# Second layer of a four-layer decoder: 258 and then 256 token columns, where 272 were computed, behind its mixer

## What is computed

```python
def conv_ffn(h, w_up, conv_w, conv_b, w_down):          # FFN_CONV = 3 taps
    u = causal_depthwise_conv(h @ w_up, conv_w) + conv_b
    gate, up = u[..., :FFN_DIM], u[..., FFN_DIM:]       # FFN_DIM = 2816
    return (jax.nn.silu(gate) * up) @ w_down

def first_block(...):
    hs = jnp.concatenate([pad, meta, x], 1)             # 48 zero rows, 16 meta, 256 tokens
    for i in range(DEPTH):                              # DEPTH = 2
        a_in = rms_norm(hs, norm_w[i, 0])
        mix = gated_deltanet(...) if i % N_MIXERS == 0 else mlstm(...)
        hs = hs + keep * rms_norm(mix, norm_w[i, 1])
        f = conv_ffn(rms_norm(hs, norm_w[i, 2]), ...)
        hs = hs + keep * rms_norm(f, norm_w[i, 3])
    return hs[:, N_PAD + N_META:]                       # only the 256 tokens of x
```

## Time and profile before

| | |
|---|---|
| median of 3 runs | 1613.73 us (1612.49 to 1618.56) |
| the profiled execution | 1615.01 us |
| its span, first to last instruction | 1612.9 us |
| TensorE matmul busy | 1500.3 us, 93% |
| TensorE weight loads busy | 1437.5 us, 89% |
| VectorE busy | 1052.0 us, 65% |
| ScalarE busy | 802.5 us, 50% |
| GpSimd busy | 253.7 us, 16% |
| mean granted TensorE clock | 0.958 |
| moved by DMA | 222.54 MB, mean 138 GB/s |

### The profile page before, as it was taken

How to read it: one execution, slowest core, us unless ns; L and a number is a source line. 1 busy time by engine, 2 the same in 40 slices (tenths; PEclk the granted TensorE clock), 3 DMA queues, 4 the chain that set the end, 5 groups by cost and what they waited for, 6 DMA issues and landing times.

```text
span 1612.9 us, 32565 instructions
## 1 busy us (share of the span) xinstructions
PE 1500.3 (93%) x11741; PEld 1437.5 (89%) x11741; DVE 1052.0 (65%) x1769; ACT 802.5 (50%) x1390; POOL 253.7 (16%) x307
## 2 busy tenths in 40 slices
PE   6999969899999999999999998999999956999997
PEld 5997868698999989898999988999999945999996
DVE  4884874647887367558886377666656663666654
ACT  5655532436655365456664354454444642454443
POOL 0202200201554000002553000021100001021100
PEclk9998976999999999999999999999999975999998
DMA  5552320053555535233655542455554710265551
GB/s 199 180 172 75 102 69 1 1 170 107 192 175 179 172 107 179 92 118 120 193 170 182 173 141 92 144 172 183 184 180 142 225 40 0 92 194 183 182 182 53
DMA packets 61141, 222.54 MB, mean 138 GB/s; under 512 B 6784, under 2 KB 7808, under 8 KB 60672
## 3 DMA queue, kind: packets, MB, share of 16 engines
q1 hardware_dynamic: 60912, 220.17, 42.6%
q10 hardware_dynamic: 144, 1.18, 0.2%
HBM read 220.28 MB, written 1.05 MB: 137 GB/s over the span
## 4 chain that ended last, share of the span: by engine, by line
PE 81%; DVE 10%; ACT 6%; issue 2%; DMA 1%; POOL 0%; ACTq 0%; DVEq 0%; SPq 0%
PE bank L396 22%; PE bank L397 21%; PE bank L398 21%; DVE wlo L377 2%; ACT whi L372 2%; PE bank L415 1%; PE bank L416 1%; PE bank L422 1%; PE bank L561 1%; PE bank L1875 1%; ACT sq L578 1%; PE bank L1216 1%; DMA par<-params 1%; PE bank L1196 1%; DVE y L2113 1%
## 5 line engine op out<-in xcount | busy, mean ns | idle before, releaser
L377 DVE TENSOR_TENSOR wlo<-raw,whi 128x1024 fp32r<-128x1024 f32 x412 | 515.8, 1253 | 308.7 <-ACT whi L372 307.4
L372 ACT ACTIVATE whi<-raw 128x1024 fp32r<-128x1024 f32 x412 | 434.5, 1056 | 377.0 <-PE bank L398 363.7
L396 PE MATMUL bank<-xs,whi 128*128 128x272 f32 (+2 forms) x2080 | 600.1, 289 | 13.6 <-DVE wlo L377 11.9
L397 PE MATMUL bank<-xs,whi 128*128 128x272 f32 (+2 forms) x2080 | 595.6, 286 | 0.0
L398 PE MATMUL bank<-xs,wlo 128*128 128x272 f32 (+2 forms) x2080 | 593.3, 285 | 0.0
L396 PEld LDWEIGHTS bank<-xs,whi 128*128 128x128 f32 x2080 | 394.1, 189 | 18.0 <-issue 13.4
L398 PEld LDWEIGHTS bank<-xs,wlo 128*128 128x128 f32 x2080 | 394.8, 190 | 0.0
L397 PEld LDWEIGHTS bank<-xs,whi 128*128 128x128 f32 x2080 | 394.5, 190 | 0.1
L396 PE MATMUL bank<-hf,whi 128*128 (+2 forms) x1024 | 293.9, 287 | 10.9 <-issue 5.0
L397 PE MATMUL bank<-hf,whi 128*128 (+2 forms) x1024 | 292.9, 286 | 0.0
L398 PE MATMUL bank<-hf,wlo 128*128 (+2 forms) x1024 | 292.5, 286 | 0.0
(11 more groups left out here) (454 smaller groups left out, 1489.9 us busy)
## 6 DMA issues: line engine op xcount, KB each, us to landing
raw<-stream SPq DMA_DIRECT2D x412, 512.0 KB, 3.6
con<-consts SPq DMA_DIRECT2D x1, 1284.5 KB, 7.8
big<-mla ACTq DMA_DIRECT2D x1, 1152.0 KB, 5.5
hs_sb<-hs SPq DMA_DIRECT2D x1, 1088.0 KB, 5.1
y_out<-hs_sb SPq DMA_DIRECT2D x8, 128.0 KB, 2.0
par<-params SPq DMA_DIRECT2D x1, 644.0 KB, 8.9
```

The costliest lines, as they stand in the source:

```text
L372: nc.scalar.activation(whi[:, s, :], raw[:, s, :], ACT.Copy).then_inc(hi_split, 1)
L377: nc.vector.tensor_tensor(wlo[:, s, :], raw[:, s, :], whi[:, s, :].bitcast(F32), ALU.subtract).then_inc(block_split, 1)
L396: nc.tensor.matmul(out_, whi[:, slot, w], hi, start=start, stop=False)
L397: nc.tensor.matmul(out_, whi[:, slot, w], lo, start=False, stop=False)
```

## The change

The second layer's parts behind its mixer leave out columns that nothing reads later. `FIRST_TOKEN` gives a first column to three phases: 14 to `ml_out` and `up1` (the 256 tokens and the two that the convolution looks back to), 16 to `down1`. Matmuls, norms, splits and the residual addition around them take the columns from there to 271. From the SiLU on, and for GpSimd's product and split, it is 16 to 271. All tensors keep their places and sizes: the operands start at a later column of the same rows. For every other phase the first column is 0. The matmuls of `keep_clock` keep their size and read columns that start at 16.

Counted in the two programs, every engine has as many instructions as before and in the same order; only the widths of the ones above differ (on TensorE 1056 + 192 matmuls from 272 to 258 columns and 528 from 272 to 256, beside the sums).

```diff
+    CONV_HALO = 2
+    FIRST_TOKEN = {"ml_out": N_META - CONV_HALO, "up1": N_META - CONV_HALO, "down1": N_META}
+    POST_FIRST = {"post0": 0, "post1": 0, "post2": FIRST_TOKEN["ml_out"], "post3": FIRST_TOKEN["down1"]}
+    PRE_FIRST = {"pre1": 0, "pre2": 0, "pre3": FIRST_TOKEN["up1"]}
+    FFN_FIRST = (0, FIRST_TOKEN["up1"], 0, 0)
+    FFN_OUT = (0, FIRST_TOKEN["down1"], 0, 0)
+
+    def cols(phase):
+        return slice(FIRST_TOKEN.get(phase, 0), width(phase))
...
     def rhs_out(g, phase):
-        return bank[g % 8][:, 0:width(phase)]
+        return bank[g % 8][:, cols(phase)]
...
-                last = three(rhs_out(g, phase), (b0 + j) % SLOTS, k, xs[:, k, 0:T], xs[:, KC + k, 0:T], k == 0, k == KC - 1)
+                last = three(rhs_out(g, phase), (b0 + j) % SLOTS, k, xs[:, k, T], xs[:, KC + k, T], k == 0, k == KC - 1)
...
-        T = T1 if b0 < FIRST_BLOCK["ev_in"] else T2
+        T = cols(phase)
...
-                last = three(rhs_out(g0 + m, phase), (b0 + k) % SLOTS, m, hf[:, up + at, 0:T], hf[:, up + lo, 0:T], k == 0, k == n - 1)
+                last = three(rhs_out(g0 + m, phase), (b0 + k) % SLOTS, m, hf[:, up + at, T], hf[:, up + lo, T], k == 0, k == n - 1)
...
-            nc.scalar.activation(sq[:, m, :], bank[(g - 8 + m) % 8][:, 0:T1], ACT.Square).then_inc(*S("norm", "act").mark(f"{name}_{m}"))
+            nc.scalar.activation(sq[:, m, lo:T1], bank[(g - 8 + m) % 8][:, lo:T1], ACT.Square).then_inc(*S("norm", "act").mark(f"{name}_{m}"))
...
-        nc.vector.tensor_tensor(hs[:, m, :], hs[:, m, :], y[:, m, :], ALU.add).then_inc(*v.mark(f"{name}_h{m}"))
+        nc.vector.tensor_tensor(hs[:, m, t], hs[:, m, t], y[:, m, t], ALU.add).then_inc(*v.mark(f"{name}_h{m}"))
...
-                ins = nc.vector.scalar_tensor_tensor(o[:, tap:T1], bk[:, 0:T1 - tap], w[:, taps - 1 - tap:taps - tap],
-                                                     o[:, tap:T1], ALU.mult, ALU.add)
+                ins = nc.vector.scalar_tensor_tensor(o[:, lo + tap:T1], bk[:, lo:T1 - tap], w[:, taps - 1 - tap:taps - tap],
+                                                     o[:, lo + tap:T1], ALU.mult, ALU.add)
...
-                u = tiles[a][0][:, 0:T]
-                nc.vector.tensor_tensor(u, u, rs[:, 0, 0:T], ALU.mult).then_inc(*st.mark(f"u{f}_{base}_{j}{a}"))
+                u = tiles[a][0][:, FFN_FIRST[f]:T]
+                nc.vector.tensor_tensor(u, u, rs[:, 0, FFN_FIRST[f]:T], ALU.mult).then_inc(*st.mark(f"u{f}_{base}_{j}{a}"))
...
-            nc.tensor.matmul(bank[g % 8][:, 0:T2], hf[:, lo, 0:P], hf[:, lo + 1, 0:T2], start=True, stop=True)
+            nc.tensor.matmul(bank[g % 8][:, 0:T2], hf[:, lo, t:t + P], hf[:, lo + 1, t:t + T2], start=True, stop=True)
```

More of the change, by code:

```diff
@@ L402, in pe_tiles @@
         b0, n = FIRST_BLOCK[phase], count or COUNT[phase]
-        T = width(phase)
+        T = cols(phase)
         mm = nc.tensor.matmul
@@ L414, in pe_tiles @@
                         pe.wait_ge(bank_free, g0 + j + 1)
-                    mm(o, whi[:, s, w], xs[:, k, 0:T], start=(k == 0), stop=False)
-                    mm(o, wlo[:, s, w], xs[:, k, 0:T], start=False, stop=False)
+                    mm(o, whi[:, s, w], xs[:, k, T], start=(k == 0), stop=False)
+                    mm(o, wlo[:, s, w], xs[:, k, T], start=False, stop=False)
             if k:
@@ L421, in pe_tiles @@
                 for j in range(AHEAD):
-                    last = mm(rhs_out(g0 + j, phase), whi[:, (b0 + j) % SLOTS, w], xs[:, KC + k - 1, 0:T], start=False, stop=(k == KC))
+                    last = mm(rhs_out(g0 + j, phase), whi[:, (b0 + j) % SLOTS, w], xs[:, KC + k - 1, T], start=False, stop=(k == KC))
                     if k == KC:
@@ L496, in pe_sum, with act_scale @@
         last.then_inc(*S("norm", "pe").mark(name))
-    def act_scale(act, name, g, dst, T, count, eps):
+    def act_scale(act, name, g, dst, T, count, eps, lo=0):
         act.wait_ge(*S("norm", "pe").at(name))
-        nc.scalar.activation(dst, bank[g % 8][:, 0:T], ACT.Ln, bias=eps, scale=1.0 / count).then_inc(bank_free, 1)
+        nc.scalar.activation(dst, bank[g % 8][:, lo:T], ACT.Ln, bias=eps, scale=1.0 / count).then_inc(bank_free, 1)
         act.wait_ge(bank_free, 8 + g + 1)
@@ L546, in build, with keep_clock, sums_pe @@
     FIRST_SUM = 3
-    def keep_clock(pe, g, n, lo=0):
+    def keep_clock(pe, g, n, lo=0, t=0):
         pe.wait_ge(bank_free, g + 1)
         for _ in range(n):
-            nc.tensor.matmul(bank[g % 8][:, 0:T2], hf[:, lo, 0:P], hf[:, lo + 1, 0:T2], start=True, stop=True)
-    def sums_pe(pe, name, src, g, parts, T):
+            nc.tensor.matmul(bank[g % 8][:, 0:T2], hf[:, lo, t:t + P], hf[:, lo + 1, t:t + T2], start=True, stop=True)
+    def sums_pe(pe, name, src, g, parts, T, lo=0):
         for m, first, last_one in parts:
@@ L560, in sums_pe @@
             pe.wait_ge(*S("norm", who).at(mark))
-            last = nc.tensor.matmul(bank[g % 8][:, 0:T], ones, ap, start=first, stop=last_one)
+            last = nc.tensor.matmul(bank[g % 8][:, lo:T], ones, ap, start=first, stop=last_one)
         if last_one:
@@ L565, in post_src @@
     def post_src(name):
+        lo = POST_FIRST[name]
         def src(m):
-            return ("dve", f"{name}_sum{FIRST_SUM - 1}", sq[:, 0, :]) if m == 0 else ("act", f"{name}_{m}", sq[:, m, :])
+            return ("dve", f"{name}_sum{FIRST_SUM - 1}", sq[:, 0, lo:T1]) if m == 0 else ("act", f"{name}_{m}", sq[:, m, lo:T1])
         return src
@@ L677, in last_act, with conv_first @@
                 split_hi(act, fourth("ev_in"))
-    def conv_first(steps_, tag, tiles, taps, a):
+    def conv_first(steps_, tag, tiles, taps, a, lo=0):
         bk, slot, w = tiles[a]
@@ L685, in conv_first, with conv_rest @@
             args["bias"] = w[:, taps:taps + 1]
-        nc.scalar.activation(cv[:, slot, :], bk[:, 0:T1], ACT.Identity, **args).then_inc(*steps_.mark(f"{tag}{a}"))
-    def conv_rest(dve, steps_, first, tag, tiles, i, taps):
+        nc.scalar.activation(cv[:, slot, lo:T1], bk[:, lo:T1], ACT.Identity, **args).then_inc(*steps_.mark(f"{tag}{a}"))
+    def conv_rest(dve, steps_, first, tag, tiles, i, taps, lo=0):
         for tap in range(1, taps):
@@ L776, in pair @@
             if f < 2:
-                conv_rest(dve, st, a_, f"f{f}_{base}_{j}", tiles, i, 3)
+                conv_rest(dve, st, a_, f"f{f}_{base}_{j}", tiles, i, 3, FFN_FIRST[f])
                 split_lo(dve, b0 + t + 1 + TAIL, ii)
@@ L787, in ffn_pool @@
     def ffn_pool(pool, f, g0):
-        st, T = S("ffn", "pool"), T1 if f < 2 else T2
+        st, t = S("ffn", "pool"), slice(FFN_OUT[f], T1 if f < 2 else T2)
         def pair(j, i, base):
```

60 lines of the change are left out of this document (32 added, 28 removed).

## The result

The changed kernel takes 1604.3 us (median of 6 runs, 1600.8 to 1605.3) against 1613.3 us for the kernel before (6 runs, 1609.5 to 1618.6): a ratio of 0.9938, with a 95% interval of 0.9921 to 0.9955. Measured a second time, against 19 runs of the kernel before, it is 1602.0 us and 0.9948, 0.9930 to 0.9966. The forecast was 1601.8 us, 0.9926 of the 1613.73 us then known for the kernel before, with a range of 1597.0 to 1608.5. Both measurements lie in the range. The gain by the medians is 9.0 us the first time and 10.7 the second, the forecast was 11.9; the two ratios, which are not the ratios of the medians, put it at 10.0 and 8.4 us. So the times alone fix the gain to some 2 us. The forecast set 0.5% as the bound of "no change" and gave 0.82 to more: both ratios lie beyond it, at 0.62% and 0.52%, but both intervals reach across it.

A forecast was written before the change was run, and what follows sets the result against it. TensorE was taken to bound the kernel, matmul distance following width. 6.3 + 3.3 + 1.2 + 0.75 + 0.35 = 11.9 us, taken from the median 1613.73, gave 1601.8 us, range 1597.0 to 1608.5.

The forecast's parts named there:

- What bounds: Whole kernel: TensorE bounds, busy 1500.3 of 1612.9 us and 81% of the chain, so fewer matmul columns shorten the end.
- `up1`, 6.3 forecast: Second layer's up projection, steady part: 272 to 258 columns, 125.70 to 119.40 us, 6.4 ns for each of 987 matmuls.
- `down1`, 3.3 forecast: Second layer's down projection: 272 to 256 columns, 66.90 us for 531 matmuls against the fourth layer's 63.60, 3.3 us less.
- `ml_out` and the passages: `ml_out`: 192 matmuls from 272 to 258 columns, 1.2 us; passage behind it 0.75 us, passage behind `down1` 0.35 us.
- The clock rival: Low-clock stretches shift as work behind `down1` comes earlier: 1.5 us each; three more give 1607 us, chance 5%.
- the third layer's stages keep their lengths to 0.3 us: Sign that the forecast is right: the first and third layers' stages stay as long as before, to 0.3 us.
- Weight loads as the pace: Rival: weight loads, not columns, pace the matmuls; only VectorE's share, some 0.5 us, is saved: 1613.2 us, chance 4%.
- VectorE as the bound: Rival: in `up1` VectorE's period stays at 6.02 us, the gain of 6.3 is gone: 1608.1 us, halfway 1605; chance 8%.
- The forecast of about 0.2 us of idle time a pair: In `up1` VectorE would still wait for TensorE, by about 0.2 us instead of 0.41 in each two-tile period.
- Operands from column 14 on: `ml_out` and `up1`: forecast no cost; rival: operands off a row's start slow 1248 matmuls, about 1729 us, chance 3%.

The follow-up runs named there:

- `down_only`: Against the kernel before, only `down1` and the norm behind it (and the SiLU and GpSimd's work) take 256 columns, the rest 272 again: 1608.6 us, 0.9977.

## Why the prediction was right, and where its sizes were off

- *What bounds.* Right. The distance between matmuls follows the columns between 272 and 256, and TensorE is busy for 98% of the changed `up1` and over 99% of `down1` (93% of `ml_out`, with the idle time at its head).
- *`up1`, 6.3 forecast, 5.5 measured.* This is the largest mis-sized term, and waits at the head of the stage are all of it. In the timelines the mean distance behind the first 96 matmuls is 125.28 ns before and 119.44 after, and 119.44 in `up2` as well: 5.84 ns a matmul, not 6.4, or 5.75 us over 984. What the first 96 take beyond that pace is 2.4 us before, 2.6 after and 1.8 in `up2`. So `up2`, taken as the future of `up1`, brought 0.6 us of fewer waits with it, and `up1`'s own waits grew by 0.2. The changed kernel's `up2` has one wait for `wlo`, 1.6 us; `up1` has two, 1.9 us in all before and 2.1 after, because the convolution puts VectorE's second block split behind it. A narrower matmul does not shorten a wait for another engine; it reaches the wait earlier. The earlier trace rows showed the two waits; I took the whole window and did not set them against the other stage's. The sum that the rows before gave by busy time alone, 123.78 - 117.84 = 5.9 us, would have been nearer.
- *`down1`, 3.3 forecast, 3.7 measured.* The same error with the other sign: `down2` and `down3` hold 1.0 us of waits beyond their pace in their first block, `down1` 0.5 before and 0.6 after. Their wait for a bank is 0.7 us, that of `down1` 0.2 to 0.3.
- *`ml_out` and the passages.* 1.05, 0.54 and 0.32 for 1.2, 0.75 and 0.35. In `ml_out` 192 matmuls at 5.9 ns (125.1 to 119.2) are 1.13 us, and its wait at the head grew by 0.09. In the passages, which operation gave less than its price I did not separate. Taken together the terms of the sum are 0.7 us too high, and that it is no more is partly luck: 0.8 too much in `up1` stands against 0.4 too little in `down1`.
- *From 11.2 to the medians' 9.0 and 10.7.* Not a step of the change: the granted clock in `ml_in`, `ev_out` and the fourth layer's mixer, 1.5 to 2.3 us to either side in single executions. The clock rival had the right price, 1.5 us a stretch, but not the cause: it let stretches shift because everything behind `down1` comes earlier, and they differ between executions of one kernel, and in `ml_in` ahead of the change. They did not take the gain, which is 11.2 us in each of the two traces of the changed kernel. The sign "the third layer's stages keep their lengths to 0.3 us" failed by this alone, in `ev_out`.
- *The range.* Its lower end is worked out from two stretches of 1.5 us and 1.2 us of scatter, which gives 1597.6, not 1597.0; nothing hangs on it.
- *Weight loads as the pace.* Refuted at this width by `down_only` (3.7 us in a stage without convolution). But there is a floor, as this rival needs one, at 111.7 ns, only 6 to 7 ns below the changed `down1`. The Trainium skill ("TensorE: Matmul & The Clock Gate", section "Back-to-back issue gap") has 81 ns for 128 columns and 131 ns for 512 in a stream with weight loads, 0.13 ns a column between them. That fits neither side here: the runs give some 0.4 ns a column above 240 columns and none below, and 111.7 ns at 128. The section's other formula, for matmuls without weight loads between them, has a slope of 0.42 ns a column, which fits above 240, but its value does not: by it the estimate is 109 ns at 256 columns, where `down1` has 118.3.
- *VectorE as the bound.* The forecast of about 0.2 us of idle time a pair was right for the late part (0.23), and the reading of it as the whole cover was not. The shortest period is read where an engine works off a backlog, 5.52 us before, not the 5.61 that I got by taking the wait out of a period that had one.
- *Operands from column 14 on.* No cost. Behind the first 96 matmuls the mean distance is 119.44 ns in `up1`, whose operands and PSUM output begin at column 14, and 119.44 in `up2` and `up3`, whose begin at column 0. `up1`'s busy time of 118.29 us for 988 matmuls lies 0.35 above `up2`'s 117.94; by the equal distances that belongs to its second wait, not to the pace.

## What to carry to other kernels

Before a stage is priced from another stage's window, take the waits out of both: only the time at the steady pace scales with the width. Narrower matmuls pay down to a floor, here at some 240 columns for these fp32r products with a weight load each, and below it nothing more was gained. When the bounding engine gets faster, look for the backlog of the next one and for the place where it is collected, here the banks that the following stage opens all at once.

## What was not expected of the hardware

- Matmuls of 224, 192 and 128 columns, each with its own weight load of 128 columns, all follow each other at 111.7 ns; at 240, 256, 258 and 272 columns it is 112.4, 118.3, 119.2 to 119.4 and 125.1 to 125.5 ns.
- A matmul stream whose operands and output begin at column 14 keeps the same 119.44 ns as one that begins at column 0.
- A wait of 4.0 us of TensorE was followed by 3.8 us at a granted clock of 0.55, in which 19 matmuls took 1.6 us more than at the 118 ns of the rest of the stage. In `ev_out` and `ml_in` such stretches come in some executions and not in others of the same kernel, at 1.5 and 1.2 us.
